# A three-layer hybrid model on one core: compression steps spread between query-key blocks, query turning ahead of the running sums, 512-column gate blocks, first loads on two queues

## Chip, cores and metric

One core of a Trainium2 chip runs the whole program once. The metric is the device time of an execution in microseconds (us). TensorE is called PE, VectorE DVE, ScalarE ACT, GpSimd POOL and SyncE SP, as in the profile.

## What is computed

256 tokens of width 1024 pass through two layers of one kind (L0, L1) and one of another (M), all in float32:

```python
# L0, L1
x = x + 0.5 * swiglu(rms_norm(x, g1), w_gate_up, w_down)          # stages L0f1, L1f1
z = rms_norm(x, gm) @ w_in                                        # u, q, k, v (512 each), gl (2 x 1024)
gates  = sigmoid(gl + b_gate)                                     # 16 blocks of 128 columns
merged = gates[0] * (pool(u) @ w_pool) + gates[1] * (attention(rope(norm(q)), rope(norm(k)), v) @ w_attn)
x = x + merged @ w_out                                            # stages L0, L1
x = x + 0.5 * swiglu(rms_norm(x, g2), w_gate_up, w_down)          # stages L0f2, L1f2
# M: one projection feeds an mLSTM (query, key through a causal convolution of 4 taps, input and forget
# gates with running sums and a running maximum) and a three-branch attention (compressed, selected, window);
# the compressed keys and values are gelu(blocks @ w1) @ w2. Then the same gated merge, and a last
# feed-forward stage Mf with a convolution of 3 taps.
```

## The kernel before

Five engine programs are written out by hand and meet only through counted semaphores. Each weight matrix is cut into tiles of 128 rows by up to 1024 columns (512 KB); `tile_plan` (L105) is the order in which all tiles are used. SP loads them in that order into five raw buffers (`load_tile`, L445): tile j waits until tile j-5 is free, which is after its low split, or, for the tiles of the compression (`w1`, not split), after PE's use. Float32 products are made from two rounded parts: ACT copies a raw tile to `whi` (L1026), DVE subtracts it into `wlo` (L1547), and the activations are kept in the same way, high and low side by side in `hx`. `hi_upto`, `lo_upto` and `ahead` (L1019, L1542) make the splits of all tiles up to a given one, five tiles ahead of use on ACT and four on DVE.

PE computes high x high, high x low and low x high. There are two forms for a block of 128 output columns. `feat_block` (L523) keeps all in one half of a bank: 16 matmuls of 256 columns with the high weights and 8 with the low ones. `wide_block` (L543), used in the feed-forward stages, takes high and low activations together: 8 matmuls of 512 columns, and 8 of 256 for the low weights into the first half. Its two halves are added outside: ACT copies the second half out (L1115) and DVE adds the first (L1640). Before the change the gate blocks of L0, L1 and M use `feat_block`, two to a bank, and ACT takes their tanh from the bank (`gate_tanh`, L1205). Banks 0 to 3 are claimed in a ring (`banks`, L229).

The small work of the mixers (RoPE, attention, pooling, compression, mLSTM) is hung on beats: each program counts `tick()` calls at the same places, two a block, and each engine does its part of a job at a given beat, in program order. An attention job takes scores and maxima at one beat, its sums two later, the turning of its probabilities (L695) three after that. In stage M beats 1 to 14 lie in the projections `Mnq` and `Mv3`, then come:

| beats before | block |
|---|---|
| 15 to 18 | query-key blocks qk0, qk1 (`conv_in`, L982) |
| 19 to 26 | eight compression steps, one beat each (`compress_step`, L855; matmuls L865) |
| 27 to 30 | qk2, qk3 |
| 31 to 46 | projections `Mmv`, `Mmo`; then the gates |

PE turns the queries at beats 23 and 24 (`turn_q`, L833, matmuls L727), for which DVE must have added the halves of RoPE (`q_add`, L1858, at 19 and 20). At beat 19 DVE also makes the running sums of the gates (`cumulate`, L1871), which need ACT's logarithm (`logf`, L1349, beat 18, with table loads), and at 20 the running maximum (L1880); ACT's `exp_m` (L1357) at beat 21 waits for it. POOL runs through X, the query's sines, four convolutions and some memsets without beats (L2166).

At the start SP loads the halves of x's first tile one after the other and ACT loads the gain and the identity; ACT squares both halves (L1041), POOL makes the reciprocal root (L2080, L2082), DVE scales (L1565), PE turns (L520). Before that PE runs 14 matmuls on zeros (L1005).

## Time and profile before

| | |
|---|---|
| three runs | 1472.69, 1473.11, 1473.73 us (median 1473.11) |
| profiled execution | 1472.98 us; its span 1471.1 us |
| busy in the span | PE 99%, PE weight loads 87%, DVE 66%, ACT 55%, POOL 10% |
| mean granted TensorE clock | 0.996 of 2.4 GHz |
| weights and other reads | 265.36 MB from HBM, 181 GB/s |

The span runs from the first instruction to the last; times in rows count from its start. Idle time of an engine other than the one at the end of the chain costs nothing by itself. Ends of matmuls are modelled, so the start-to-start distance in the chain of waits is the measure of one, not its own duration.

### The profile page before, as it was taken

Reading aid. Unit: us, or ns where it says so; the run is one execution under the profiler, and the core shown is the slowest. Engines: PE = TensorE matmul, PEld = TensorE weight load, DVE = VectorE, ACT = ScalarE, POOL = GpSimd, SP = SyncE. Lnnn points to the kernel's source line nnn. Section 1 sums busy time; section 2 is a strip of 40 time slices with the busy share of each in tenths; the row PEclk is TensorE's granted clock in tenths of the full one; section 3 lists DMA queues with packets and bytes.
Section 4 is the critical chain, followed back from the end, with each engine's and each line's share of the span. In section 5 each row is a group of like instructions: output and inputs, shape, how many; then the busy total and the mean of one; then the engine's idle time right before and its main releaser. Section 6 shows DMA issues by size and latency. Waiting matters only on the chain.

```text
span 1471.1 us, 21418 instructions
## 1 busy us (share of the span) xinstructions
PE 1457.3 (99%) x8342; PEld 1275.5 (87%) x8342; DVE 973.9 (66%) x1562; ACT 814.2 (55%) x1394; POOL 150.8 (10%) x219
## 2 busy tenths in 40 slices
PE   8999999999999999999999999999998999999999
PEld 7888888998888888888889988888886999888887
DVE  5666676566665666666675577665667756778776
ACT  6555556644655546555566546555567555456553
POOL 0200023000000001000050004000059000100000
PEclk9999999999999999999999999999999999999999
DMA  7766555355656556566464456655546333546552
GB/s 272 256 189 196 181 203 190 130 164 179 207 183 197 187 174 211 188 189 197 161 227 142 145 171 214 191 185 198 172 147 241 118 115 130 164 167 227 190 184 99
DMA packets 73685, 267.82 MB, mean 182 GB/s; under 512 B 8176, under 2 KB 8304, under 8 KB 73456
## 3 DMA queue, kind: packets, MB, share of 16 engines
q1 hardware_dynamic: 73296, 265.85, 55.3%
q8 instruction: 67, 1.10, 0.3%
q10 hardware_dynamic: 288, 0.59, 0.1%
q14 instruction: 34, 0.28, 0.1%
HBM read 265.36 MB, written 1.05 MB: 181 GB/s over the span
## 4 chain that ended last, share of the span: by engine, by line
PE 96%; ACT 1%; DVE 1%; DMA 1%; issue 0%; POOL 0%; SPq 0%; ACTq 0%; DVEq 0%; POOLq 0%
PE bank L547 25%; PE bank L550 13%; PE bank L500 8%; PE bank L501 8%; PE bank L502 8%; PE bank L537 5%; PE bank L531 5%; PE bank L530 5%; PE bank L557 4%; PE bank L558 4%; PE bank L562 4%; PE bank L520 1%; PE bank L705 1%; PE bank L686 1%; PE bank L695 1%; PE bank L727 1%
## 5 line engine op out<-in xcount | busy, mean ns | idle before, releaser
L1547 DVE TENSOR_TENSOR wlo<-raw,whi 128x1024 fp32r<-128x1024 f32 (+1 forms) x481 | 578.6, 1226 | 22.5 <-ACT whi L1026 22.5
L1026 ACT ACTIVATE whi<-raw 128x1024 fp32r<-128x1024 f32 (+1 forms) x481 | 498.5, 1050 | 15.1 <-DMA raw<-w_dram 8.3
L547 PE MATMUL bank<-hx,whi 128*128 128x512 f32 x1600 | 398.6, 391 | 0.0
L547 PEld LDWEIGHTS bank<-hx,whi 128*128 128x128 f32 x1600 | 293.6, 188 | 56.7
L550 PEld LDWEIGHTS bank<-hx,wlo 128*128 128x128 f32 x1600 | 218.3, 190 | 15.6
L550 PE MATMUL bank<-hx,wlo 128*128 128x256 f32 x1600 | 223.1, 282 | 0.0
L500 PE MATMUL bank<-whi,hid 128*128 128x512 f32 x536 | 211.2, 394 | 0.2 <-issue 0.2
L501 PE MATMUL bank<-wlo,hid 128*128 128x512 f32 x536 | 209.9, 392 | 0.0
L502 PE MATMUL bank<-whi,hid 128*128 128x512 f32 x536 | 208.6, 389 | 0.0
L1055 ACT ACTIVATE hid<-prod 128x256 fp32r<-128x256 f32 x126 | 52.7, 418 | 170.0 <-DVE prod L1651 109.0
L502 PEld LDWEIGHTS bank<-whi,hid 128*128 128x128 f32 x536 | 100.7, 188 | 21.9
L557 PE MATMUL bank<-whi,hx 128*128 128x512 f32 (+1 forms) x288 | 116.4, 405 | 0.6 <-DVE hx L1572 0.6
L500 PEld LDWEIGHTS bank<-whi,hid 128*128 128x128 f32 x536 | 101.1, 189 | 17.9 <-issue 0.4
L501 PEld LDWEIGHTS bank<-wlo,hid 128*128 128x128 f32 x536 | 101.1, 189 | 16.2
L530 PE MATMUL bank<-hx,whi 128*128 128x256 f32 x416 | 111.8, 303 | 0.0
L558 PE MATMUL bank<-whi,hx 128*128 128x512 f32 (+1 forms) x288 | 111.6, 389 | 0.0
L531 PE MATMUL bank<-hx,whi 128*128 128x256 f32 x416 | 103.1, 282 | 0.0
L2080 POOL TENSOR_SCALAR small<-small 128x1 f32<-128x1 f32 x16 | 10.9, 684 | 885.1 <-ACT arena L1041 885.1
L1640 DVE TENSOR_TENSOR prod<-prod,bank 128x256 f32<-128x256 f32 x100 | 42.0, 420 | 89.3 <-ACT prod L1115 89.1
L1640 DVE TENSOR_TENSOR sil<-sil,bank 128x256 f32<-128x256 f32 x80 | 33.6, 420 | 97.1 <-ACT sil L1115 97.1
L1115 ACT ACTIVATE sil<-bank 128x256 f32<-128x256 f32 x80 | 30.6, 383 | 118.4 <-PE bank L550 118.4
L1577 DVE TENSOR_TENSOR hid<-prod,hid 128x256 fp32r<-128x256 f32 x126 | 53.6, 425 | 61.0 <-ACT hid L1055 61.0
(254 smaller groups left out, 1785.3 us busy)
## 6 DMA issues: line engine op xcount, KB each, us to landing
raw<-w_dram SPq DMA_DIRECT2D x486, 512.0 KB, 4.0
gain<-g_dram SPq DMA_DIRECT2D x7, 512.0 KB, 4.5
arena<-c_dram SPq DMA_DIRECT2D x2, 768.0 KB, 6.9
cst<-c_dram SPq DMA_DIRECT2D x1, 1056.0 KB, 6.0
out_dram<-x SPq DMA_DIRECT2D x4, 256.0 KB, 2.0
par<-p_dram SPq DMA_DIRECT2D x1, 867.0 KB, 7.6
raw<-w_dram SPq DMA_DIRECT2D x2, 432.0 KB, 3.2
gain<-g_dram ACTq DMA_DIRECT2D x1, 512.0 KB, 4.4
```

The source lines that it names most:

```text
L500: e.matmul(psum, shi, mhi, start=first, stop=False, skip_group_check=True)
L501: e.matmul(psum, shi, mlo, start=False, stop=False, skip_group_check=True)
L502: return e.matmul(psum, slo, mhi, start=False, stop=last, skip_group_check=True)
L530: e.matmul(psum, whj[:, w:w + P], hi(k), start=k == 0, stop=False, skip_group_check=True)
L531: e.matmul(psum, whj[:, w:w + P], lo(k), start=False, stop=False, skip_group_check=True)
L547: e.matmul(b[:, :], hi_of(j)[:, k * P:k * P + P], hx[:, k * 2 * S:k * 2 * S + 2 * S], start=k == 0, stop=False, skip_group_check=True)
L550: ins = e.matmul(b[:, 0:S], lo_of(j)[:, k * P:k * P + P], hiT(k), start=False, stop=k == KD - 1, skip_group_check=True)
L557: e.matmul(b[:, 0:n], hiT(k, a * P, a * P + P), w, start=k == 0, stop=False, skip_group_check=True)
L558: e.matmul(b[:, 0:n], loT(k, a * P, a * P + P), w, start=False, stop=False, skip_group_check=True)
L1026: e.activation(hi_of(t), raw_of(t), ACT.Copy).then_inc(sem["w_hi"], 1)
L1547: e.tensor_tensor(lo_of(t), raw_of(t), hi_of(t).bitcast(F32), ALU.subtract).then_inc(sem["w_lo"], 1)
L1640: e.tensor_tensor(dst, dst, bank[K.BANK[tag, "ab"[part], i][0]][:, 0:S], ALU.add).then_inc(sem["sum"], 1)
```

## The change

In stage M the order of tiles and blocks becomes qk0, two compression steps, qk1, three steps, qk2, three steps, qk3 (`MIXED`), on SP's loads, ACT, DVE and PE alike; the splits there run three (ACT) and two (DVE) positions ahead. PE's gate rows move from beat 17 to 16, the turning of the queries to 24 and 25, `q_add` to 22 and 23, both running sums to 24, `exp_m` to 26, the convolution ends to 32, 37, 42, 46, the fold to 8. In L0 and L1 (not in M) each gate block is a `wide_block` in a bank of its own; ACT copies the low half into the gate's place, DVE adds the high half, and ACT takes the tanh in SBUF, one block later. At the start SP loads x's first half and the identity, ACT the second half and the gain; DVE squares the second half; 15 matmuls on zeros; the first high split moves behind the first copy of the turned x. The semaphore lists are left out of the diff.

```diff
@@ -99,6 +99,8 @@
+MIXED = ([("qk", 0)] + [("w1", i) for i in range(2)] + [("qk", 1)] + [("w1", i) for i in range(2, 5)]
+         + [("qk", 2)] + [("w1", i) for i in range(5, 8)] + [("qk", 3)])
@@ -132,11 +134,8 @@
     for g, n in L2_GROUPS[:3]:
         for k, m in a_group(n):
             plan.append((f"M{g}{k}", m * n, True))
-    plan.extend((f"Mqk{f}", TW, True) for f in range(2))
-    for i in range(8):
-        plan.append((f"M{'kv'[i // 4]}w1{i % 4}", TW, False))
-    for f in range(2, 4):
-        plan.append((f"Mqk{f}", TW, True))
+    for kind, i in MIXED:
+        plan.append((f"Mqk{i}", TW, True) if kind == "qk" else (f"M{'kv'[i // 4]}w1{i % 4}", TW, False))
     for g, n in L2_GROUPS[3:]:
         for k, m in a_group(n):
             plan.append((f"M{g}{k}", m * n, True))
@@ -154,7 +153,7 @@
-CONV = (25, 34, 42, 48)
+CONV = (32, 37, 42, 46)
@@ -283,7 +282,11 @@
-                claim((f"{tag}g", f), "gate", 16 * m + 2 * f + 2)
+                if tag == "M":
+                    claim(("Mg", f), "gate", 16 * m + 2 * f + 2)
+                else:
+                    for j in range(2):
+                        claim((f"{tag}g", f, j), "g_sum", 16 * m + 2 * f + j + 1)
@@ -471,8 +474,8 @@
-            for h in range(2):
-                e.dma_start(xq(0, h), x_in[0:P, h * 512:h * 512 + 512]).then_inc(sem[f"ld_x0{h}"], 16)
+            e.dma_start(xq(0, 0), x_in[0:P, 0:512]).then_inc(sem["ld_x00"], 16)
+            e.dma_start(ident, const_in[:, 0:P]).then_inc(sem["ld_i"], 16)
@@ -540,15 +543,19 @@
                 if tick:
                     tick()
-            def wide_block(j, b):
+            def wide_block(j, b, tick=None):
                 E.wait_ge("w_hi", SI[j] + 1)
                 for k in range(KD):
                     e.matmul(b[:, :], hi_of(j)[:, k * P:k * P + P], hx[:, k * 2 * S:k * 2 * S + 2 * S], start=k == 0, stop=False, skip_group_check=True)
+                    if tick and k == 5:
+                        tick()
                 E.wait_ge("w_lo", SI[j] + 1)
                 for k in range(KD):
                     ins = e.matmul(b[:, 0:S], lo_of(j)[:, k * P:k * P + P], hiT(k), start=False, stop=k == KD - 1, skip_group_check=True)
                 ins.then_inc(sem["tile"], 1)
+                if tick:
+                    tick()
             def group_part(g, n, j, k0, m, a, b):
                 E.wait_ge("w_hi", SI[j] + 1)
@@ -810,9 +817,8 @@
-                    b = claim((f"{tag}g", f))
...
-                        feat_block(T[f"{tag}g{j}{f}"], b[:, j * S:j * S + S], tick=tick)
+                        wide_block(T[f"{tag}g{j}{f}"], claim((f"{tag}g", f, j)), tick)
@@ -963,9 +969,9 @@
                     beat += 1
                     if 10 <= beat <= 13:
                         turn_k(beat % 2, beat < 12)
-                    if beat in (23, 24):
-                        turn_q(beat - 23)
-                    if beat == 17:
+                    if beat in (24, 25):
+                        turn_q(beat - 24)
+                    if beat == 16:
                         gate_rows()
                     if beat == 29:
                         gate_cols()
@@ -985,13 +991,12 @@
-                conv_in(0)
-                conv_in(1)
-                for i in range(8):
-                    compress_step(i)
-                    tick()
-                for f in range(2, 4):
-                    conv_in(f)
+                for kind, i in MIXED:
+                    if kind == "qk":
+                        conv_in(i)
+                    else:
+                        compress_step(i)
+                        tick()
@@ -1001,7 +1006,7 @@
-            for i in range(14):
+            for i in range(15):
@@ -1202,18 +1207,28 @@
-            def gate_tanh(s, m, f):
-                tag = STAGES[s]
-                b = bank[K.BANK[f"{tag}g", f][0]]
-                E.wait_ge("tile", DONE[f"{tag}g1{f}"])
+            gate_slot = lambda f, j: gates[:, (2 * f + j) * S:(2 * f + j + 1) * S]
+            def gate_low(m, f, j):
+                E.wait_ge("tile", DONE[f"L{m}g{j}{f}"])
+                E.wait_ge("qkt_t", 4 * m + 4)
+                e.activation(gate_slot(f, j), bank[K.BANK[f"L{m}g", f, j][0]][:, S:2 * S], ACT.Copy).then_inc(sem["g_low"], 1)
+            def gate_of_sum(m, n):
+                f, j = n // 2, n % 2
...
-                if m < 2:
-                    E.wait_ge("qkt_t", 4 * m + 4)
-                else:
-                    E.wait_ge("tile", DONE["Mvw13"])
-                    E.wait_ge("qkt_t", 8 + 2)
-                    if f >= 6:
-                        E.wait_ge("ml_s", 4)
+                E.wait_ge("g_sum", 16 * m + n + 1)
+                e.activation(gate_slot(f, j), gate_slot(f, j), ACT.Tanh, scale=0.5, bias=hb16[:, j * KD + f:j * KD + f + 1]).then_inc(sem["gate"], 1)
+            def gate_tanh(f):
+                b = bank[K.BANK["Mg", f][0]]
+                E.wait_ge("tile", DONE[f"Mg1{f}"])
+                E.wait_ge("hb", 3)
+                E.wait_ge("tile", DONE["Mvw13"])
+                E.wait_ge("qkt_t", 8 + 2)
+                if f >= 6:
+                    E.wait_ge("ml_s", 4)
@@ -1320,7 +1335,10 @@
-                    gate_tanh(s, l, f)
+                        gate_low(l, f, j)
+                        if f or j:
+                            gate_of_sum(l, 2 * f + j - 1)
+                gate_of_sum(l, 2 * KD - 1)
@@ -1418,13 +1436,13 @@
                         turned_k(beat % 2, beat < 12)
                     if beat == 18:
                         logf()
-                    if beat == 21:
+                    if beat in (24, 25):
+                        turned_q(beat - 24)
+                    if beat == 26:
                         exp_m()
-                    if beat in (23, 24):
-                        turned_q(beat - 23)
                     if beat in CONV:
                         conv_end(CONV.index(beat))
-                    if beat == 26:
+                    if beat == 28:
                         compressed(0)
                     attention(2, beat, 29, js)
                     if beat in (31, 34):
@@ -1484,13 +1501,14 @@
-                conv_in(0)
-                conv_in(1)
-                for i in range(8):
-                    ahead(T[f"M{'kv'[i // 4]}w1{i % 4}"])
-                    tick()
-                for f in range(2, 4):
-                    conv_in(f)
+                for kind, i in MIXED:
+                    if kind == "qk":
+                        hi_upto(T[f"Mqk{i}"] + 3)
+                        conv_in(i)
+                    else:
+                        if i < 6:
+                            hi_upto(T[f"M{'kv'[i // 4]}w1{i % 4}"] + 3)
+                        tick()
@@ -1510,20 +1528,18 @@
-                    gate_tanh(s, 2, f)
+                    gate_tanh(f)
...
+            e.dma_start(xq(0, 1), x_in[0:P, 512:1024]).then_inc(sem["ld_x01"], 16)
...
-            e.dma_start(ident, const_in[:, 0:P]).then_inc(sem["ld_i"], 16)
...
-            squares(0, 0, 1)
+            norm_hi(0, 0, (0,))
...
-            hi_upto(0)
-            norm_hi(0, 0, (0,))
+            norm_hi(0, 0, (1,))
...
-            norm_hi(0, 0, (1,))
@@ -1828,6 +1844,9 @@
+                        g = gates[:, (2 * f + j) * S:(2 * f + j + 1) * S]
+                        E.wait_ge("g_low", 16 * l + 2 * f + j + 1)
+                        e.tensor_tensor(g, g, bank[K.BANK[f"{tag}g", f, j][0]][:, 0:S], ALU.add).then_inc(sem["g_sum"], 1)
@@ -1864,7 +1883,6 @@
-                    e.tensor_reduce(fold, ident.rearrange("p (j i) -> p i j", j=4), AX, ALU.add).then_inc(sem["c_fold"], 1)
@@ -1984,15 +2002,16 @@
                         k_norm(beat - 4)
                     if beat in (6, 7):
                         k_add(beat - 6)
+                    if beat == 8:
+                        e.tensor_reduce(fold, ident.rearrange("p (j i) -> p i j", j=4), AX, ALU.add).then_inc(sem["c_fold"], 1)
+                    if beat == 17:
+                        gate_rows()
                     if beat in (17, 18):
                         q_cos(beat - 17)
-                    if beat == 17:
-                        gate_rows()
-                    if beat == 19:
+                    if beat in (22, 23):
+                        q_add(beat - 22)
+                    if beat == 24:
                         cumulate()
-                    if beat in (19, 20):
-                        q_add(beat - 19)
-                    if beat == 20:
                         running_max()
                     if beat == 29:
                         gate_cols()
@@ -2035,13 +2053,14 @@
-                conv_in(0)
-                conv_in(1)
-                for i in range(8):
-                    ahead(T[f"M{'kv'[i // 4]}w1{i % 4}"])
-                    tick()
-                for f in range(2, 4):
-                    conv_in(f)
+                for kind, i in MIXED:
+                    if kind == "qk":
+                        lo_upto(T[f"Mqk{i}"] + 2)
+                        conv_in(i)
+                    else:
+                        if i < 6:
+                            lo_upto(T[f"M{'kv'[i // 4]}w1{i % 4}"] + 2)
+                        tick()
@@ -2055,11 +2074,13 @@
                         tick()
                 merge_tail(s, 2)
+            E.wait_ge("ld_x01", 16)
+            e.tensor_tensor_reduce(sqj[:, 512:1024], xq(0, 1), xq(0, 1), 1.0 / 1024, 0.0, ALU.mult, ALU.add, st[:, 1:2]).then_inc(sem["sq_v"], 1)
             norm_x(0, 0)
+            norm_lo(0, 0, (0,))
             lo_upto(0)
-            norm_lo(0, 0, (0,))
+            norm_lo(0, 0, (1,))
             lo_upto(1)
-            norm_lo(0, 0, (1,))
             lo_upto(2)
             norm_x(0, 1)
             lo_upto(3)
@@ -2076,7 +2097,8 @@
             def rstd(n, a):
                 c0 = st[:, 4 * a + 2:4 * a + 3]
-                E.wait_ge("sq", 4 * n + 2 * a + 2)
+                E.wait_ge("sq_v", 1)
+                E.wait_ge("sq", 4 * n + 2 * a + 1)
                 e.tensor_scalar(c0, st[:, 4 * a:4 * a + 1], st[:, 4 * a + 1:4 * a + 2], EPS, ALU.add, ALU.add).then_inc(sem["rstd"], 1)
                 E.wait_ge("rstd", 4 * n + 2 * a + 1)
                 e.tensor_tensor(c0, c0, mhalf[:, 0:1], ALU.pow).then_inc(sem["rstd"], 1)
```

## Rows read from the trace of the kernel before

**Rows 1.** The page, busy time of each engine over the span
```profile
PE 1457.3 (99%) x8342; PEld 1275.5 (87%) x8342; DVE 973.9 (66%) x1562; ACT 814.2 (55%) x1394; POOL 150.8 (10%) x219
```

**Rows 2.** PE's waits over the span, longest first: total us, times, longest
```profile
PE bank L727 <- DVE gates L1861: 4.6, 1, 4.6
```

**Rows 3.** Chain of waits, end of L0's gate blocks: start, us, what
```profile
302.01 0.96 PE bank L537 x8
304.89 0.96 PE bank L537 x8
```

**Rows 4.** Chain of waits, last feed-forward stage: two wide blocks in a row
```profile
1360.07 1.81 PE bank L547 x8
...
1364.67 0.95 PE bank L550 x8
```

**Rows 5.** The page, groups: line, engine, op, shapes, count | busy, mean ns | idle before
```profile
L1547 DVE TENSOR_TENSOR wlo<-raw,whi 128x1024 fp32r<-128x1024 f32 (+1 forms) x481 | 578.6, 1226 | 22.5 <-ACT whi L1026 22.5
L1026 ACT ACTIVATE whi<-raw 128x1024 fp32r<-128x1024 f32 (+1 forms) x481 | 498.5, 1050 | 15.1 <-DMA raw<-w_dram 8.3
...
L1640 DVE TENSOR_TENSOR sil<-sil,bank 128x256 f32<-128x256 f32 x80 | 33.6, 420 | 97.1 <-ACT sil L1115 97.1
L1115 ACT ACTIVATE sil<-bank 128x256 f32<-128x256 f32 x80 | 30.6, 383 | 118.4 <-PE bank L550 118.4
```

**Rows 6.** Windows, L0's gate stage: length, busy per engine, clock, DMA share, GB/s
```profile
249.00:309.00 60.00, 60.00 (x480) 59.08 (x479) 33.87 (x86) 37.73 (x81) 0.00 (x0) 1.00 0.46 148
```

**Rows 7.** Timeline of DVE, one attention job of L0: start, us, instruction, idle before
```profile
264.57 0.35 DVE L1710 TENSOR_SCALAR arena<-arena,small 128x256 f32<-128x256 f32 x1
268.03 0.29 DVE L1690 CUSTOM_DVE_ANT_0 arena<-bank,cst 128x128 f32<-128x128 f32 x1 [3.11 <-PE bank L686]
```

**Rows 8.** Timeline of PE, the turning of that job's probabilities
```profile
270.70 0.49 PE L695 MATMUL bank<-cst,arena 128*128 128x128 f32 x3
```

**Rows 9.** Timeline of PE, compression steps, turning of queries, third query-key block
```profile
1104.58 2.37 PE L865 MATMUL bank<-raw,gates 128*32 128x256 f32 x40
1111.58 0.99 PE L727 MATMUL bank<-cst,gates 128*128 128x128 f32 x4 [4.63 <-DVE gates L1861]
...
1115.83 0.39 PE L530 MATMUL bank<-hx,whi 128*128 128x256 f32 x1
```

**Rows 10.** Timeline of DVE, running sums and query additions
```profile
1108.17 0.94 DVE L1873 SCALAR_TENSOR_TENSOR prod<-prod,sil 4x256 f32<-4x256 f32 x1 [3.34 <-ACT sil L1355]
...
1110.85 1.27 DVE L1861 TENSOR_TENSOR gates<-gates 128x512 f32<-128x512 f32 x2
...
1113.18 0.77 DVE L1884 TENSOR_TENSOR sil<-sil,prod 4x256 f32<-4x256 f32 x1
```

**Rows 11.** Windows, the microsecond after the wait (columns as in rows 6)
```profile
1112.00:1113.00 1.00, 1.00 (x11) 0.37 (x9) 1.00 (x2) 0.00 (x0) 0.92 (x2) 0.50 1.01 414
```

**Rows 12.** Timeline of SyncE's queue: the next weight loads issued
```profile
1105.28 1.37 SPq L453 DMA_DIRECT2D raw<-w_dram  x2
```

**Rows 13.** DMA issues, 1095 to 1135 us: KB each, median us to landing
```profile
raw<-w_dram SPq DMA_DIRECT2D x17, 512.0 KB, 4.8
```

**Rows 14.** Timeline of POOL: the clearing of the compressed-score tile
```profile
1140.99 0.30 POOL L2231 MEMSET arena<- 128x256 f32 x1
```

**Rows 15.** Timeline of DVE: first use of that tile
```profile
1144.62 0.40 DVE L1912 TENSOR_TENSOR arena<-bank,small 128x240 f32<-128x240 f32 x1
```

**Rows 16.** Chain of waits, the start: start, us, what
```profile
1.16 4.80 DMA x<-x_dram
...
6.89 0.31 POOL small L2080
...
11.09 0.80 PE bank L557
```

**Rows 17.** Timeline of ACT, the start: first square
```profile
5.00 0.63 ACT L1041 ACTIVATE arena<-x 128x512 f32<-128x512 f32 x1 [1.86 <-DMA x<-x_dram]
```

**Rows 18.** Windows, the start (columns as in rows 6)
```profile
12.00:16.00 4.00, 4.00 (x11) 3.03 (x11) 3.18 (x5) 2.61 (x6) 0.88 (x2) 0.50 0.95 354
```

10 lines of the change are left out of this document (4 added, 6 removed).

## The prediction, made before any run of the change

> **What bounds the kernel now.** I read the busy times first: TensorE (PE) is busy 99% of the span [rows 1]. So what can change the time is either PE's own work per block or the few places where PE stands still. The list of PE's waits comes second: its head is one wait of 4.6 us, at the turning of the queries in the third mixer (stage M) [rows 2]. Third come the chain in a gate stage, which gives the cost of a gate block, and the same chain in a feed-forward stage, which already uses the block form that the change brings to the gates [rows 3, 4]. Last come timelines around the long wait and around the start. Everything else in the 1471 us is untouched.
>
> **Part 1, gate blocks (stages L0 and L1).** A gate block is 24 matmuls of 256 columns; it starts every 2.88 us, 304.89 - 302.01 [rows 3], or 0.120 us a matmul. The wide form is 8 of 512 and 8 of 256. Two such blocks in a row take from 1360.07 to 1365.62 (1364.67 plus 0.95), so 2.775 each [rows 4]. The columns are the same 6144; what goes is eight instructions, each with its gap. There are 8 x 2 blocks in each of two stages, so 32 x (2.88 - 2.775) = 3.4 us, all of it on the chain, since PE does nothing else there and never waits. Bounds: 0 (no gain) and 3.8 (a tenth more, for a mean read off two blocks).
> The rows say that a 256-column matmul costs 13 ns more than 256 columns at 2.4 GHz (106.7 ns), and the 512-column one, 1.81/8 = 226 ns, also 13 ns more. The Trainium skill, "TensorE: Matmul & The Clock Gate", section "Wait — 56ns, not 53.3ns?", gives a fixed cost of about 2.5 ns a matmul on the warm array; by that, dropping eight matmuls in each of 32 blocks would bring an estimated 0.6 us and not 3.4. The trace has the duration, so the trace's figure is taken.
> What it adds: for each of the 32 blocks a copy of the low half from PSUM on ScalarE (ACT), 0.383 us, and a VectorE (DVE) addition, 0.420 [rows 5]; the tanh stays, reading SBUF. That is 6.1 us of ACT and 6.7 us of DVE in each stage of about 60 us, where ACT was busy 37.7 and DVE 33.9 [rows 6]: 73% and 68% after. I cost it at nothing. The cover is this: a bank is claimed again four blocks later, 11 us, and copy, addition and hand-offs need about 1.2; behind the new waits stand, on ACT the exponentials and splits of the next block, on DVE the splits (made four to five tiles ahead) and the maxima and sums of attention. In the old trace one job's scaling ended at 264.92 and PE turned the probabilities of that job at 270.70, 5.8 us later, while DVE idled 3.11 us in the same job [rows 7, 8]. If that cover goes, each of the 16 jobs pays.
>
> **Part 2, stage M.** Eight compression steps ran in one row between query-key blocks 1 and 2. Five of them take 2.37 us, 0.47 each; then PE idles 4.63 until 1111.58 and runs at a granted clock of 0.50 afterwards, 1.2 GHz, until about 1115.83 [rows 9, 11]. Work that took 4.25 us at half clock is 2.1 us at the full one. So 4.63 + 2.1 = 6.7 us were lost here; that is the most this part can give.
> The wait has two causes. On DVE the sum that PE waits for stood behind the running sums: DVE idled 3.34 us for ACT's logarithm, then took from 1108.17 to 1110.85 before it reached the additions [rows 10]. And the sixth step's tile could only be loaded when step one had freed its buffer: issued at 1105.28, with 4.8 us to landing, so there at 1110.1 [rows 12, 13]. Removing only the first cause would bring 1.5 us. The change removes both: additions at beats 22 and 23, running sums at 24, queries turned at 24 and 25, and the steps spread as 2, 3, 3, so that a 2.88 us block stands between groups.
> What is late next, counted from the end of the first step (0) with raw tiles landing 4.8 after they are asked for, a split of 1.05 on ACT and 1.23 on DVE [rows 5]. Step five's tile is asked for at 0 and lands at 4.8; PE gets there after 0.47 + 2.88 + 0.94 = 4.3: wait 0.5. Block qk2's tile is asked for at 0.47 and is split at 0.47 + 4.8 + 1.05 = 6.3; PE is there at 4.8 + 0.47 = 5.3: wait 1.0. DVE reaches the first addition only behind qk2's low split, 1.23 + 0.64 = 1.9 after that split's start; PE wants to turn after half the block, 1.44: wait 0.45. The running sums (2.7 us from 1108.17 to 1110.85, and after the two additions, 1.27, until 1113.18 + 0.77, so 1.8 more [rows 10]) and ACT's exponential end about 0.3 after PE asks for the gate columns. Together 2.3 us of new waits, none long, so no fall of the clock: gain 6.7 - 2.3 = 4.4. Every step's DMA is counted: the same 512 KB tiles in another order on SyncE's queue, none added. Bounds: 1.5 (only the first cause helps) and 6.7.
> GpSimd does not get earlier: its four convolutions run until it clears the compressed-score tile at 1140.99, done at 1141.29, and DVE first uses that tile at 1144.62 [rows 14, 15]. With PE 4.4 us earlier DVE would stand there for 1.1 us, with sums of one attention job and splits behind it; these have several us of slack, so I take nothing and keep 1.1 for the range. The later convolution ends (beats 32, 37, 42, 46) are still ahead of the first use at beat 45; moving them, the fold and the exponential issues nothing new.
>
> **Part 3, the start.** The second half of x landed at 1.16 + 4.80 = 5.96, the first by 5.00, and GpSimd began the norm at 6.89 after two squares on ACT [rows 16, 17]. Now both halves are issued at once from two queues and DVE squares the second. A 512-column square took ACT 0.63 [rows 17]; I take 0.8 for DVE, accumulator included. If both land at 5.0, GpSimd starts at 5.8; if only the issue is saved (0.43), the half lands at 5.5 and GpSimd starts at 6.35. From there to the first real matmul the chain took 4.2 us (11.09 - 6.89 [rows 16]), and takes as long after, as tile 0's split now stands behind the first copy. So 0.5 to 1.1 earlier. Until 16 us the clock was at 0.50 [rows 18]; if it rises at the same moment, half of that is given back. Taken: 0.7; bounds 0.2 and 2.6, the latter if less idling keeps the clock up (the 12 to 16 us stretch, 4 us of PE work at 0.50, would shrink to about 2, and 0.6 more from before it).
> The Trainium skill, "Trainium Kernel Development and Optimization", section "Key Constraints", says that DMAs of several issuing engines share the same 16 DMA engines and that issuing from two saves only issue time; this speaks against a full microsecond here, and by it alone the estimate would be the later of the two starts, 6.35.
>
> **Sum.** 3.4 + 4.4 + 0.7 = 8.5 us off the profiled execution's 1472.98: 1464.5. The median of the runs shown is 1473.11, 0.13 away; I give 1464.4. The measurement tells 0.2%, about 3 us, from no change.
>
> **Rivals.**
> A, the forecast: 1464.4, with 1462.5 to 1466.5 as its own range. Chance 0.57.
> B, new waits take most of stage M: buffers free in time but landings slip behind each other, or the 1.1 us at the cleared tile reaches PE. Gain 1.5 there: 1467.4. For it: five raw buffers only, GpSimd's end fixed. Against: DMA was idle before the steps. 0.15.
> C, more than counted: all 6.7 in stage M and 2.6 at the start: 1472.98 - 12.7 = 1460.3. For it: the clock did fall in both places. 0.14.
> D, the gates save nothing, as the per-matmul gap goes with columns or ports: 1467.9. By the skill's 2.5 ns a matmul named above it would be near this. Against: the same form at 2.775 in this very trace [rows 4]. 0.05.
> E, the change does not do what it says: gates as in D, and stage M's long wait only moves to a later beat (GpSimd's end at 1141 holds the same moment), leaving 0.7: 1472.3. 0.05.
> F, slower: DVE and ACT become the bound in the gate stages. Place: PE's turning of probabilities, behind the new additions. It decides once the hand-offs eat the 5.8 us of a job [rows 7, 8]; to lose at all the 16 jobs would have to pay 8.5/16 = 0.5 us each. At 1.0 each: 1464.5 + 16 = 1480.5. Against: 1.5 additions a job are 0.6 us where DVE idled 3.11. 0.04.
>
> **How the numbers follow.** The likeliest is A. The range 1460.0 to 1468.9 takes in C, B and D, and leaves out E and F. Faster: A + B + C + D = 0.91; same: E, 0.05; slower: F, 0.04.
>
> **What would show it.** Gate blocks: 512-column matmuls and 256-column ones at 2.77 us a block, no PE wait in those stages. Stage M: the 4.63 us wait gone, three or four below 1.2 us on raw tiles, splits and the query sum, granted clock 1.00 throughout. Start: GpSimd's first norm step at 5.8 to 6.35, the first wide matmul near 10.3. I am wrong if PE waits in the gate stages, if a wait above 2 us stands in stage M, or if the blocks still take 2.88.

## The result and the profile after

The changed kernel takes 1469.03 us (median of 10 runs, 1465.51 to 1471.76) against 1472.57 for the kernel before (10 runs, 1471.78 to 1473.73): ratio 0.9973, 95% interval 0.9964 to 0.9982. That is 3.5 us faster where I forecast 8.5, and 0.13 us above the top of my range. The profiled run took 1468.62 us, its span 1466.8 (before: 1472.98 and 1471.1). Its runs lie 6 us apart, those of before 2.

The busy times of all engines from the page, which answer to [rows 1]:

```profile
PE 1453.1 (99%) x8088; PEld 1259.9 (86%) x8088; DVE 984.1 (67%) x1596; ACT 822.9 (56%) x1424; POOL 150.0 (10%) x219
```

PE's waits over the whole span of the changed kernel (total us, times, longest), answering to [rows 2]. The 4.6 at the turning of the queries is 1.1 now; two waits above 2 us stand beside it, for ScalarE's split of a raw tile (L533) and for the scaled probabilities of an attention job (L702). Both are in stage M.

```profile
PE bank L702 <- DVE arena L1726: 2.8, 2, 2.6
PE bank L533 <- ACT whi L1031: 2.6, 2, 2.1
PE bank L564 <- ACT whi L1031: 1.4, 2, 1.1
PE bank L734 <- DVE gates L1880: 1.1, 1, 1.1
```

**The gates did what was forecast, a third smaller.** The chain of waits at the end of L0's gate blocks (start, us, what), for [rows 3]; then the window over the gate stage (columns as in rows 6), and VectorE's additions in the view that groups instructions by line:

```profile
300.12 1.84 PE bank L550 x8
...
302.92 1.84 PE bank L550 x8
```

```profile
249.00:309.00 60.00, 60.00 (x369) 53.70 (x368) 38.17 (x102) 42.59 (x96) 0.00 (x0) 1.00 0.43 146
```

```profile
L1849 DVE TENSOR_TENSOR gates<-gates,bank 128x256 f32<-128x256 f32 x16 | 6.7, 419 | 16.4 <-ACT gates L1216 16.4
```

A block starts every 2.79 us, 302.92 - 300.12 = 2.80 and the ones beside it 2.78 and 2.79, against 2.88. PE is busy for all of the 60 us: ACT at 42.6 and VectorE (DVE) at 38.2 make it wait nowhere. From the start of L0's first gate block to the end of its last, the chain takes 57.85 us (247.85 to 305.70) against 59.01 (249.72 to 308.73).

**The start gave more than forecast.** The timeline from 4.6 us on, for [rows 16, 17], and the windows that answer to [rows 18]:

```profile
4.62 0.69 DVE L2078 CUSTOM_DVE_ANT_0 arena<-x 128x512 f32<-128x512 f32 x1 [4.62 <-DMA x<-x_dram]
...
5.50 0.30 POOL L2102 TENSOR_SCALAR small<-small 128x1 f32<-128x1 f32 x1 [4.54 <-DVE small L2078]
...
9.74 0.47 PE L564 MATMUL bank<-whi,hx 128*128 128x512 f32 x1 [1.12 <-ACT whi L1031]
```

```profile
8.00:12.00 4.00, 2.87 (x13) 1.83 (x13) 3.06 (x4) 3.71 (x7) 0.00 (x0) 1.00 1.03 420
12.00:16.00 4.00, 3.67 (x15) 1.88 (x13) 3.05 (x4) 2.50 (x4) 0.87 (x2) 1.00 0.91 320
```

The second half of x is squared from 4.62, GpSimd (POOL) starts at 5.50 (6.89 before), the first wide matmul at 9.74 (11.09 before), and the clock is at 1.00 from 12 to 16 us, where it was at 0.50.

**Stage M gave next to nothing on balance.** One window over the same 55 us, the kernel before and then after:

```profile
1090.00:1145.00 55.00, 48.68 (x361) 40.73 (x360) 37.70 (x68) 35.99 (x73) 47.56 (x64) 0.97 0.57 202
```

```profile
1090.00:1145.00 55.00, 48.60 (x352) 41.37 (x351) 38.00 (x73) 37.58 (x74) 43.64 (x57) 0.97 0.55 193
```

PE is busy for 48.68 and 48.60 us, at a mean clock of 0.97 in both. So the new waits add up to as much as the long one and the small ones beside it did. PE's timeline after:

```profile
1105.22 0.38 PE L533 MATMUL bank<-hx,whi 128*128 128x256 f32 x1 [2.13 <-ACT whi L1031]
...
1108.02 0.66 PE L734 MATMUL bank<-cst,gates 128*128 128x128 f32 x4 [1.11 <-DVE gates L1880]
...
1112.45 0.38 PE L533 MATMUL bank<-hx,whi 128*128 128x256 f32 x1 [0.47 <-ACT whi L1031]
...
1126.87 0.55 PE L702 MATMUL bank<-cst,arena 128*128 128x128 f32 x3 [2.60 <-DVE arena L1726]
```

Together 6.3 us. When PE reached its first query-key block in stage M (1093.44 against 1097.58) it was 4.1 us ahead of before, at the first tile of the mv group (1117.04 against 1123.22) 6.2, and at the end of the span 4.3: what the new order won, the wait at 1126.87 and the clock behind it took back. The windows (columns as before; the last three are clock, DMA share and GB/s):

```profile
1090.00:1095.00 5.00, 5.00 (x43) 5.00 (x42) 1.78 (x3) 4.74 (x12) 4.35 (x7) 1.00 0.03 11
1095.00:1100.00 5.00, 4.92 (x49) 3.86 (x48) 2.25 (x5) 2.87 (x9) 4.92 (x12) 1.00 0.16 46
1100.00:1105.00 5.00, 3.09 (x38) 2.12 (x37) 0.00 (x0) 3.36 (x6) 4.84 (x8) 1.00 0.93 317
1125.00:1130.00 5.00, 3.13 (x18) 2.70 (x19) 4.83 (x15) 4.18 (x9) 4.68 (x5) 0.78 0.59 188
1130.00:1135.00 5.00, 5.00 (x24) 4.17 (x23) 4.96 (x10) 3.15 (x10) 4.61 (x6) 0.88 0.52 181
```

After the last wait, while PE works, the clock falls: 5 x 0.22 + 5 x 0.12 = 1.7 us of full-speed work lost. Ahead of the first one, DMA is all but idle for 10 us and then at 0.93. The chain of waits says why; the first fence is the third query-key block (qk2), the second the attention job:

```profile
1097.52 1.10 PE bank L871 x16
...
1098.64 5.45 DMA raw<-w_dram
...
1104.11 1.07 ACT whi L1031
...
1106.76 1.22 DVE gates L1880
```

```profile
1116.76 1.77 DVE wlo L1563
...
1119.20 0.64 DVE small L1713
...
1119.86 0.59 ACT arena L1180 x2
...
1121.30 0.96 ACT whi L1031
...
1123.43 1.77 DVE wlo L1563
...
1125.72 0.83 DVE arena L1725
...
1126.87 0.55 PE bank L702 x3
```

A compression step ends at 1098.62. It frees one of five raw buffers, the load of qk2's weights goes into it and takes 5.45 us to land, ACT splits it in 1.07, PE has had nothing to do since 1103.1. In the second fence two splits by DVE come before the maxima of the first attention job (1119.20), ACT's exponentials wait for those, three more splits of ACT and three of DVE (the last two wait for ACT's) come before its sums and scaling (1125.72), and PE waits until 1126.87.

VectorE's pace is part of this wait. Its two splits in the fence took 1.77 each where 1.22 is usual, the step that joins the maxima 0.64 where the same form took 0.16 in L0, the scaling 0.83 where the same line took 0.29 in L0: 0.55 + 0.48 + 0.55 + 0.54 = 2.1 us on a chain that ends in a wait of 2.60. Beside each of them lies an instruction of GpSimd's convolutions; beside those in L0 lies none. In the whole trace of the changed kernel 15 of the 481 low splits took over 1.24 us. All 15 began while a GpSimd TENSOR_TENSOR was running, and 14 of them ended 1.08 or 1.09 us after it ended. The kernel before has such splits too, so this is not what the change added, and no run here was made without the convolutions.

### The profile page after: what moved, and what is told of

Read it like the earlier page. It is cut to its first block, busy times and chain, and to the rows that moved or that the text cites. A ratio compares the mean times of both kernels' runs of the same rounds, so it can differ in the third digit from the quotient of the medians.

```text
span 1466.8 us, 20973 instructions
## 1 busy us (share of the span) xinstructions
PE 1453.1 (99%) x8088; PEld 1259.9 (86%) x8088; DVE 984.1 (67%) x1596; ACT 822.9 (56%) x1424; POOL 150.0 (10%) x219
## 3 DMA queue, kind: packets, MB, share of 16 engines
HBM read 265.36 MB, written 1.05 MB: 182 GB/s over the span
## 4 chain that ended last, share of the span: by engine, by line
PE 97%; ACT 1%; DMA 1%; DVE 1%; issue 0%; SPq 0%; DVEq 0%
PE bank L550 29%; PE bank L555 15%; PE bank L503 8%; PE bank L504 8%; PE bank L505 8%; PE bank L564 4%; PE bank L565 4%; PE bank L569 4%; PE bank L540 3%; PE bank L534 3%; PE bank L533 3%; PE bank L523 1%; PE bank L712 1%; DMA raw<-w_dram 1%; PE bank L693 1%; PE bank L702 1%
## 5 line engine op out<-in xcount | busy, mean ns | idle before, releaser
L550 PE MATMUL bank<-hx,whi 128*128 128x512 f32 x1856 | 470.4, 394 | 0.0
L550 PEld LDWEIGHTS bank<-hx,whi 128*128 128x128 f32 x1856 | 339.7, 188 | 64.5
L555 PEld LDWEIGHTS bank<-hx,wlo 128*128 128x128 f32 x1856 | 253.0, 190 | 18.4
L555 PE MATMUL bank<-hx,wlo 128*128 128x256 f32 x1856 | 258.6, 282 | 0.0
L569 PE MATMUL bank<-wlo,hx 128*128 128x512 f32 (+1 forms) x288 | 87.8, 387 | 0.1
L1120 ACT ACTIVATE prod<-bank 128x256 f32<-128x256 f32 x100 | 38.3, 383 | 86.3 <-PE bank L555 85.6
```

The source lines that it names most:

```text
L550: e.matmul(b[:, :], hi_of(j)[:, k * P:k * P + P], hx[:, k * 2 * S:k * 2 * S + 2 * S], start=k == 0, stop=False, skip_group_check=True)
L555: ins = e.matmul(b[:, 0:S], lo_of(j)[:, k * P:k * P + P], hiT(k), start=False, stop=k == KD - 1, skip_group_check=True)
L569: ins = e.matmul(b[:, 0:n], hiT(k, a * P, a * P + P), w, start=False, stop=k == KD - 1, skip_group_check=True)
L1120: e.activation(dst, bank[K.BANK[tag, "ab"[part], i][0]][:, S:2 * S], ACT.Copy).then_inc(sem["low"], 1)
```

## The experiments

Gain is against the kernel before on the same chip (medians 1473.09 for the first four, 1473.17 for the next four, then 1472.92 and 1472.67). A row rests on 5 to 11 runs. Two intervals contain 1: the old stream order and the misplaced fill are not told apart from the kernel before.

| kernel | median us (lowest to highest) | gain | ratio, 95% interval |
|---|---|---|---|
| gates alone | 1470.83 (1470.23 to 1471.21) | 2.3 | 0.9985 (0.9976 to 0.9993) |
| start alone | 1470.66 (1469.06 to 1471.52) | 2.4 | 0.9983 (0.9974 to 0.9992) |
| stage M alone | 1470.22 (1468.43 to 1473.08) | 2.9 | 0.9985 (0.9976 to 0.9994) |
| stage M, old stream order | 1472.17 (1469.78 to 1473.06) | 0.9 | 0.9993 (0.9984 to 1.0002) |
| the change again | 1469.38 (1466.54 to 1470.07) | 3.8 | 0.9971 (0.9960 to 0.9983) |
| shorter splits ahead | 1471.10 (1467.14 to 1473.46) | 2.1 | 0.9986 (0.9977 to 0.9995) |
| change with fill | 1468.65 (1466.46 to 1469.44) | 4.5 | 0.9966 (0.9952 to 0.9979) |
| shorter, with fill | 1471.20 (1468.52 to 1472.49) | 2.0 | 0.9985 (0.9977 to 0.9994) |
| gates and start | 1468.58 (1467.04 to 1469.07) | 4.3 | 0.9969 (0.9956 to 0.9981) |
| gates and stage M | 1471.05 (1467.66 to 1472.40) | 1.9 | 0.9980 (0.9972 to 0.9989) |
| start and stage M | 1469.91 (1467.33 to 1471.12) | 3.0 | 0.9980 (0.9971 to 0.9989) |
| gates, start, misplaced fill | 1471.57 (1470.45 to 1472.81) | 1.4 | 0.9993 (0.9984 to 1.0002) |
| change, half loads | 1465.51 (1465.38 to 1466.03) | 7.2 | 0.9951 (0.9939 to 0.9963) |
| gates, start, half loads | 1468.30 (1468.15 to 1468.85) | 4.4 | 0.9971 (0.9959 to 0.9982) |
| gates, start, fill | 1467.65 (1466.81 to 1468.83) | 5.0 | 0.9967 (0.9955 to 0.9979) |
| old stream order, half loads | 1470.91 (1470.05 to 1472.22) | 1.8 | 0.9989 (0.9980 to 0.9998) |

**1. The parts alone.** Each is the kernel before with one part of the diff.

```diff
 gates: in L0 and L1
-feat_block(T[f"{tag}g{j}{f}"], b[:, j * S:j * S + S], tick=tick)
+wide_block(T[f"{tag}g{j}{f}"], claim((f"{tag}g", f, j)), tick)
```

> The gate blocks of L0 and L1 alone. Theory 1 (gap per matmul): the profile of the whole change shows blocks starting every 2.79 us instead of 2.88, so 32 x 0.09 = 2.9 us faster, minus a few tenths where a block resumes behind attention's small matmuls; 2.3 to 3.0 faster, with the same spread of times as the kernel before (about 2 us between lowest and highest). Rival (the gates cause the wide spread of times): lowest and highest lie 4 us or more apart.

```diff
 start: x's second half on ScalarE's queue, its square on VectorE
+e.dma_start(xq(0, 1), x_in[0:P, 512:1024]).then_inc(sem["ld_x01"], 16)
```

> The start alone. Theory 1 (the clock of the start decides): GpSimd's norm begins at 5.5 instead of 6.9 us; in executions where the granted clock falls at the start as before, 0.3 to 1 us faster, and where it stays at 1.00, 1.8 to 3 us faster, so times in two groups and a mean clock near 0.9985 (only stage M's fall left) or 0.996. Rival (the start is a fixed shift of 1.8 us, as the one profile shows): all times 1.8 us lower and close together.

```diff
 stage M: MIXED, CONV, split distances, beats of the sums and of turn_q
-CONV = (25, 34, 42, 48)
+CONV = (32, 37, 42, 46)
```

> Stage M alone. The profile of the whole change shows 6.3 us of PE waits in stage M against 6.3 before, and a fall of the clock behind the last of them. Theory 1 (the wait only moved to beat 34): no more than 1 us faster, and 2 us faster in executions where the clock does not fall. Rival (stage M gains its 4.4 us when PE does not arrive early from the other parts): 3 to 5 us faster.

Gates 2.3 with runs 1 us apart, start 2.4 with runs 2.5 apart, stage M 2.9 with runs 4.6 us apart. Sum 7.6, whole 3.5: the parts do not add, and by the intervals this gap is clear of the noise. The start's clock stayed at 1.00 in it alone too, so its gain doesn't need the other parts.

**2. Stage M without the new stream order.**

```diff
 against stage M alone
-MIXED = ([("qk", 0)] + [("w1", i) for i in range(2)] + [("qk", 1)] + [("w1", i) for i in range(2, 5)]
-         + [("qk", 2)] + [("w1", i) for i in range(5, 8)] + [("qk", 3)])
+MIXED = [("qk", 0), ("qk", 1)] + [("w1", i) for i in range(8)] + [("qk", 2), ("qk", 3)]
```

> Stage M as in e3, but the eight compression steps again in one row between blocks 1 and 2: only the additions, sums and beats are in the new order. Theory 1 (two causes, the sixth step's load the second): PE waits at the sixth step on a raw tile until about 5 us after the first step's end, 3 us or more, with a fall of the clock; the time is within 1.5 us of the kernel before. Rival (the running sums were the only cause): as fast as e3 or faster.

Its gain of 0.9 is not clear of zero. PE now waits for the landing itself (its waits between 1090 and 1145 us):

```profile
PE bank L863 <- DMA raw<-w_dram: 3.3, 2, 1.7
```

So the second cause of the old wait that I named is real: with the queries out of the way, the steps wait for their own tiles. This is read from one profile.

**3. The wait at beat 34, and the clock.** c_after is the change once more, on the chip of the next three.

> The changed kernel again, unchanged, as the reference for the other three on one chip. Theory 1 (clock falls in stage M make the spread): 1465.5 to 1472 once more, lower times with a higher mean clock. Rival (the first session was a chance): close to the sum of the three parts, 7.5 us below the kernel before.

Its runs, like those of the result, are fast when the clock holds: at a mean clock of 1.000 they took 1466.54 and 1467.58, at 0.996 they took 1470.01 and 1470.07. Its profiled execution is one of the fast ones (1467.58), and the clock stayed at 1.00 in stage M although PE waited 3.0 us there for the same scaled probabilities, and 1.7 for the split of qk2. So a wait of that length is followed by a fall of the clock in one execution and not in another.

```diff
 ScalarE and VectorE in the mv group: splits less far ahead (ScalarE's part; VectorE's has lo_upto and 2, 3, 4, 4)
-group_ticks("Mmv", 512)
+for (k0, _), far in zip(a_group(512), (3, 4, 5, 5)):
+    hi_upto(T[f"Mmv{k0}"] + far)
+    tick()
+    tick()
```

> The changed kernel, with the splits ahead of the first part of Mmv cut from five and four tiles to three and two, and back to five and four by the third. Theory 1 (catching up with splits in front of the first attention sums makes PE late at beat 34): the 2.6 us wait at the first turning of probabilities falls under 0.8 us, and the median is 2 to 4 us below that of the changed kernel. Rival (GpSimd, or weight loads that land late, make it late): that wait stays above 1.5 us.

```diff
 TensorE: matmuls that no result depends on, 14 ahead of qk2 and 12 at beat 34
+for _ in range(n):
+    e.matmul(b[:, 0:S], hx[:, 0:P], hiT(0), start=True, stop=True, skip_group_check=True)
```

> The changed kernel, with 14 throw-away matmuls (1.7 us) of PE in front of query-key block 2 and 12 (1.4 us) at beat 34, at the two places where PE waited 2.1 and 2.6 us. They write to banks that are overwritten afterwards. Theory 1 (PE's idling there lowers the clock, and the lowered clock makes the spread): no fall in stage M, mean clock 1.000 in nearly all executions, spread under 2 us, median near 1466. Rival (the spread comes from the order in which other engines and DMAs meet): spread as in the changed kernel, median up to 3 us higher.

> The shorter split distance together with the 14 matmuls in front of query-key block 2 alone. Theory 1: the fastest of the four, 1463 to 1465, close together. Rival: no better than the shorter distance alone.

The last is both edits, with the 14 alone. Splitting less far ahead removed the wait at beat 34 and put a longer one some beats later, for the tile into which DVE spreads the compressed values. Its median is 1.7 us above that of the change, with runs 6 us apart; it is no faster, and whether it is slower these runs do not settle. Timeline of PE of that kernel:

```profile
1133.88 0.88 PE L702 MATMUL bank<-cst,arena 128*128 128x128 f32 x3 [3.48 <-DVE arena L1924]
```

The fill kept the clock (1.000 in 4 of 5 runs, 0.999 in the fifth), yet the median fell by only 0.7 us, which 5 and 6 runs do not tell from nothing. In its profiled execution the same load, behind the same step, took 7.09 us to land.

```profile
1098.35 7.09 DMA raw<-w_dram
```

PE's 14 extra matmuls lay ahead of qk2, and it still waited 1.91 us for the split (timeline of the same kernel):

```profile
1106.57 0.39 PE L533 MATMUL bank<-hx,whi 128*128 128x256 f32 x1 [1.91 <-ACT whi L1039]
```

So keeping the clock up is not enough: with it at 1.000 this kernel took 1466.46 to 1468.76. What the fill itself costs, 26 matmuls of 0.12 us that only in part lie in waits, is not separated from what it saves.

**4. Pairs.**

> The gate part and the start together, stage M as it was before. If the two parts add, the time is that of before minus 2.3 minus 2.4, 1468.4 on the scale of 1473.1, with a ratio of 0.9968, and stage M keeps its 4.6 us wait for the turned queries with the fall of the clock after it. The whole change stands at 1469.0 to 1469.4, so that its stage M would then be worth nothing or up to 1 us of loss on top of these two. The rival, that each early stage's gain is partly lost again in stage M whatever M looks like (M's waits are for work that does not start earlier), gives 1470 or more, and a wait in M longer than 4.6.

> The gate part and stage M, the start as before. Additive parts give 1473.1 minus 2.3 minus 2.9, 1467.9. If the gates' shorter blocks take from stage M what it needs (its raw landings and splits come no earlier, so the two new waits before the third query-key block and at beat 34 grow), it is 1469.5 to 1470.5, no faster than stage M alone with half the gates' gain, and the two longest waits are above the 1.4 us each of stage M alone.

> The start and stage M, the gates as before. Additive parts give 1473.1 minus 2.4 minus 2.9, 1467.8. The start lies 1080 us ahead of stage M and can only reach it as a shift of everything, so that I expect this pair to add, within 0.7 us; if the loss lies between gates and mixer, this pair has waits of 1.4 us and less in stage M, as stage M alone. If it is as far short as the pair of gates and mixer (1469.5 or more), the loss does not come from the gates, and the fall of the clock, which comes in some runs and not in others, is the likelier cause.

Gates and start add: 4.3 of 4.7. Stage M, worth 2.9 on the kernel before, is worth 0.6 on top of the start (3.0 - 2.4), nothing on top of the gates (1.9 - 2.3) and nothing on top of both (3.5 to 3.8 against 4.3). Each gain is uncertain by some 1.3 us and a difference of two by up to 2, so no pair decides by itself; all three fall the same way, and gates and start without stage M have a median no higher than the whole change. The runs of gates and stage M fall into two groups, five of 1467.66 to 1469.11 at a mean clock of 0.998 and six of 1471.05 to 1472.40 at 0.994 to 0.997, so its median says how often the clock fell as much as what the parts are worth. My expectation that start and stage M would add was wrong, so the loss isn't the gates' alone. What I can see that differs in the profiles is how long qk2's load takes from its issue. In stage M alone, chain of waits:

```profile
1101.65 4.26 DMA raw<-w_dram
...
1105.93 1.06 ACT whi L1024
```

4.26 us, and the wait was 0.9; in the pair with the gates 5.08 and 1.8, in the pair with the start 5.45 and 2.1, in the whole 5.45 and 2.1. Each is one profiled execution, that of gates and stage M from the faster group.

**5. Loads.** In the next three the eight compression tiles load 512 of their 1024 columns. PE multiplies whatever the rest of the buffer holds, so these kernels do not compute the compressed keys and values; they only test the loads.

```diff
+m = TW // 2 if name[0] == "M" and "w1" in name else n
-e.dma_start(raw_of(j), wstream[off * P:(off + n) * P].rearrange("(p n) -> p n", p=P))
+e.dma_start(raw_of(j)[:, 0:m], wstream[off * P:(off + n) * P].rearrange("(p n) -> p n", p=P)[:, 0:m])
```

> The whole change, but each of the eight compression tiles loads only half its columns (256 KB for 512 KB); TensorE multiplies whatever the other half of the buffer holds, so the compressed keys and values differ from the reference's. If stage M is bound by loads (the ring of five buffers, 8 us without a load, then 5.5 us to the landing of the third query-key block), that block's wait for its split falls from 2.1 us to below 0.7, the later splits come earlier and the time falls by 2 to 4 us against the whole change, to 1465.5 to 1467. If it is bound by the serial steps of ScalarE and VectorE, the wait moves and the time stays within 1 us of 1469.

> Gates and start with stage M as before, and the same half loads for the compression tiles. Here the chain goes through the log sums and the additions of the queries on VectorE, not through a landing: the 4.6 us wait stays, and the time is within 1 us of the 1468.6 of gates and start. If loads bind the old order too, it falls by 2 us or more.

> Stage M's edits with the stream in its old order, gates and start as before (that run gave 1472.2, with TensorE waiting 3.3 us for landings of compression tiles), now with the half loads. If the landings are the whole second cause, both waits go and the time falls by 3 us and its clock share, to 1467 to 1469; if the wait only moves to a split or to VectorE, it falls by less than 1.5 us.

In the new order the half loads bring 3.4 to 3.6 us by gains, and the spread of 6 us shrinks to 0.65, with a mean clock of 1.000 in four of five runs. In the old order of tiles and of beats, with gates and start, they bring nothing (gains of 4.4 and 4.3). So the changed stage M depends on its loads and the old one did not. With the new beats and the old stream order they bring 0.8 by gains, not clear of zero and less than the 3 I expected: PE's wait for landings halves to 1.7, and one of 2.0 for a split stands behind it. Chain, then PE's waits between 1090 and 1145 us, of the whole change with half loads:

```profile
1098.20 4.86 DMA raw<-w_dram
...
1103.08 1.06 ACT whi L1032
```

```profile
PE bank L534 <- ACT whi L1032: 2.0, 2, 1.5
PE bank L703 <- DVE arena L1727: 1.2, 1, 1.2
```

The landing still takes 4.86, PE waits 1.5 for the split instead of 2.1, and 1.2 at beat 34 instead of 2.6. Between the two profiles PE's waits of this stretch fall from 6.3 to 5.0 and 1.7 us of lost clock are gone, so more than half of what stage M gained goes through the clock: at a clock of 1.000 the change with full loads took 1465.51 to 1467.58 in four runs, against 1465.38 to 1466.03 here.

**6. The clock behind the old wait.** Fill in the old stage M, with gates and start. The first kernel has the condition as printed, the second has a == 0.

```diff
 def turn_q(a):
     E.wait_ge("kc2_ev", 4 * a + 4)
+    if a:
+        for _ in range(32):
+            e.matmul(side[a][:, 0:S], hx[:, 0:P], hiT(0), start=True, stop=True, skip_group_check=True)
     E.wait_ge("rp_add", 10 + a + 1)
```

> Gates and start with stage M as before, and 32 throw-away matmuls of 256 columns that no result depends on, ahead of the turning of the second half of the queries, where TensorE waits 4.6 us. If half-speed matmuls after that wait cost the 2.1 us that the windows show, this takes them back: 2.1 below the run of gates and start, 1466.3 if that is 1468.4, with a granted clock of 1.00 in 1110 to 1120 us. It would then beat the whole change by about 3 us. If the clock falls at another wait behind it (the waits of beats 34 and later, about 0.8 each before), or if the throw-away matmuls end later than the queries are ready, the gain is under 1 us.

> Gates and start with stage M as before, and 32 throw-away matmuls ahead of the turning of the first half of the queries, where the 4.6 us wait stands (the run before had them at the second half, behind the wait, where they cost 3.0 us). The wait falls to 0.8 us, the clock stays at 1.00 from 1105 to 1115 us, and the 2.1 us of half-speed work behind the wait come back: 1466.5 against the 1468.6 of gates and start, with clocks of 1.000. If what follows waits for loads anyway, less than 1 us comes back.

The first is misplaced: the 4.6 us wait stands at the first half of the queries, so 32 matmuls (3.8 us) came behind it and cost 3.0. The second has them in the wait. Gates and start with the old stage M, windows, then the same with the fill; between them PE's wait for the queries in the one with the fill:

```profile
1105.00:1110.00 5.00, 2.30 (x13) 1.16 (x14) 4.89 (x8) 0.83 (x1) 4.58 (x5) 0.55 0.89 351
1110.00:1115.00 5.00, 5.00 (x40) 3.52 (x40) 3.03 (x4) 4.33 (x6) 4.66 (x5) 0.76 0.60 220
```

```profile
PE bank L735 <- DVE gates L1885: 0.6, 1, 0.6
```

```profile
1105.00:1110.00 5.00, 4.35 (x45) 2.74 (x44) 4.49 (x6) 0.68 (x3) 4.62 (x5) 1.00 0.88 341
1110.00:1115.00 5.00, 4.00 (x33) 4.00 (x34) 3.76 (x3) 3.88 (x7) 4.74 (x4) 1.00 0.80 256
```

The clock stays at 1.00 where it was 0.55 and 0.76. The mean over these windows counts the idle part too, and a slow clock costs nothing while PE stands still, which it did until 1107.7. Windows of 1 us show a clock of 0.50 from there to 1112.4, about 4.7 us of PE work, so 2.3 us were lost. Of these 0.9 us reach the end (1468.58 to 1467.65; 0.7 by gains; not clear of zero). With the fill PE arrives earlier at qk2 and waits there for its split, which it did not without:

```profile
1111.00 0.39 PE L534 MATMUL bank<-hx,whi 128*128 128x256 f32 x1 [1.00 <-ACT whi L1036]
```

This version has the lowest median of those that compute everything, 5.0 us below before against 3.5 to 3.8 for the change; the runs do not tell the two apart.

## Why the prediction was wrong

- **Gates, 3.4 forecast, 2.3 measured.** Right in mechanism. The term was mis-sized at both ends of its difference: a block takes 2.79, not 2.775, and 16 blocks save 59.01 - 57.85 = 1.16 in L0, where the forecast had 16 x 0.105 = 1.7 and 16 x 0.09 would be 1.4. The cover for ACT's copies and DVE's additions held in full. By the 2.5 ns a matmul of the Trainium skill ("TensorE: Matmul & The Clock Gate", section "Wait — 56ns, not 53.3ns?") the estimate was 0.6; the trace does not agree, and the measured 2.3 decides.
- **Start, 0.7 forecast, 2.4 measured**, near the top of its bounds (2.6). Both halves landed by 4.62, earlier than the 5.0 I took, POOL started at 5.50 and not 5.8, and the first wide matmul came 1.35 us earlier. The rest, about 1.05 by subtraction, is what the clock gave back of the 2.5 us that PE's 5 us at 0.50 had cost: I named "less idling keeps the clock up" as the bound and gave it too little weight. By the Trainium skill's rule that two queues save only issue time ("Trainium Kernel Development and Optimization", section "Key Constraints") GpSimd would have started at an estimated 6.35; the trace has 5.50. That does not refute the rule: the change also put the 512 KB load of the gain behind x's half on ScalarE's queue, where it had been first, and no run separates the two.
- **Stage M, 4.4 forecast, 2.9 alone and nothing in the whole.** This is the step that failed, in three places. First, "raw tiles landing 4.8 after they are asked for": 4.8 was a median over loads that were not alike. In the same trace of before the one issued at 1095.66 took 3.4, and those behind the first compression step took longer one after the other (issues of 1105 to 1106, 1106 to 1107 and 1107 to 1109 us):

```profile
raw<-w_dram SPq DMA_DIRECT2D x2, 512.0 KB, 4.2
raw<-w_dram SPq DMA_DIRECT2D x2, 512.0 KB, 5.3
raw<-w_dram SPq DMA_DIRECT2D x3, 512.0 KB, 6.4
```

qk2's is the next one behind the first after such a pause, and took 4.26 to 7.09 from profile to profile. The wait for it was 2.1, not 1.0; half a microsecond of that is the wait of 0.5 that I had put on step five's tile, which did not come. Second, I ended the list of what is late next at the gate columns. Behind them stands the chain of maxima, exponentials, splits and scaling, and PE waited 2.60 at its end. Third, "none long, so no fall of the clock": the clock fell in most runs. With it at 1.000 the change took 1465.51 and 1465.75 (in the second set of runs 1466.54 and 1467.58), with 0.996 1470.72 and 1471.76. So where I added up 2.3 us of new waits, the window of 55 us has 6.3 of waits and 1.7 of lost clock, 8.0 together. The kernel before has 6.3 of waits there (the 4.6 and small ones) and 2.1 of lost clock, 8.4.
- **The two additions of the queries** wait 1.1 and not 0.45: they took 2.23 us, against 1.27 for the same two before, and the low split ahead of them 1.63, where I had 1.23.

```profile
1106.76 2.23 DVE L1880 TENSOR_TENSOR gates<-gates 128x512 f32<-128x512 f32 x2
```

GpSimd's timeline beside them, the kernel before and then after:

```profile
1110.73 1.88 POOL L2204 TENSOR_TENSOR arena<-arena,par 128x256 f32<-128x256 f32 x1
```

```profile
1105.83 1.58 POOL L2228 TENSOR_TENSOR arena<-arena 128x256 f32<-128x256 f32 x1
1107.50 0.94 POOL L2226 TENSOR_TENSOR arena<-arena,par 128x256 f32<-128x256 f32 x1
```

The same lines of GpSimd took 0.61 and 0.73 elsewhere. Before, GpSimd's was the one that took longer, by 1.27, just what the two additions lasted. After, its instruction had been running since 1105.83 and ended at 1107.41, and the first addition, begun at 1106.76, ended only behind it. I had taken VectorE's times from rows and put nothing for GpSimd beside it.

- **GpSimd's end**, which I costed at nothing, cost nothing: its clearing of the tile moved from 1140.99 to 1136.28 with the rest, and no wait names it. What I left out is what its convolutions do to VectorE on the way, as shown above.
- **Rivals.** B, "new waits take most of stage M", is the outcome, and I gave it 0.15 and a gain of 1.5 in stage M; they took all. Its reason, "landings slip behind each other", holds for the first wait; the longest stands behind the attention job. C's clock at the start came true as well, and the start brought 1.7 us more than I had taken. It is luck, then, that the time came out only 0.13 us above the range: on top of gates and start, stage M was off by 5.2 us (3.5 - 4.3 = -0.8 where I had 4.4). My own sign of error, "a wait above 2 us in stage M", was met twice.

What stays open: why the same load, asked for in the same place, lands in 4.3 us in one profile and in 7.1 in another. In both profiles the weight loads are on the queue, beside them 0.03 MB of instructions. In the three microseconds after the first the queue moved 254 to 291 GB/s in the slow case (1099 to 1102) and 336 to 426 in the fast one (1103 to 1106), at a DMA share of 0.72 to 0.90 and 0.97 to 1.04. That the parts do not add is shown by 7.6 against 3.5; that it is stage M which loses its gain when it is reached some 2 us earlier is what the medians of all pairs point to, none of them clear of the noise. That the landing is the reason fits the single profiles and the run with half loads, but how much is the landing, how much GpSimd beside VectorE and how much the clock is not separated.

## What to carry to other kernels

When a long wait has two causes, one on an engine and one in the loads, price what takes its place from the ring of buffers at that point: how long the ring was full and idle, how many loads start at once when it opens, how long each of those took in the trace (not the median of all), and how many tiles of work lie between the release of a slot and the use of its next content. Follow the chain behind the removed wait until an engine shows idle time, not to the next wait only. And test the parts in pairs: two parts that are good alone can be worth only one of them together.

## What the runs showed of the hardware that was not expected

- One 512 KB load, in the same place of the same queue, took from 4.26 to 7.09 us to land in seven profiles; in the whole change the DMA share was 0.93 around it. In the kernel before, such loads took 3.4 us alone and 4.2 to 6.4 in a row behind a pause.
- Two additions of 128 x 512 took 2.23 us at 1106.76, and 1.27 in the kernel before [rows 10]. GpSimd was busy for about nine tenths of either stretch. In the second case it was GpSimd's instruction that took longer, 1.88 where its line takes 0.61. Of the changed kernel's splits 15 of 481 low splits took over 1.24 us, all 15 begun while a GpSimd TENSOR_TENSOR ran, and 14 ended 1.08 or 1.09 us behind its end. This is read from traces; no run took GpSimd's work away.
- Throw-away matmuls in a wait of 4.6 us kept the granted clock at 1.00, but of 2.3 us of work lost to the clock only 0.9 came back, and PE waited 1.0 for the next split. The clock that a window shows counts idle time too; only the part in which PE works costs anything.
